# First stage of a two-layer decoder kernel rewritten: pooling bands and weight units take turns, and the router's preparation is spread over the engines

## What is computed

```python
def rmsnorm(x, g):
    y = xf * lax.rsqrt(jnp.mean(xf * xf, axis=-1, keepdims=True) + EPS)
    return (y * g).astype(x.dtype)

def pool_mixer(x, pool_w, pool_scale):          # 4 groups of 512 columns, windows 2, 4, 8, 16
    for gi, w in enumerate(POOL_WINDOWS):
        ...
        outs.append((c - c_prev) / cnt - xf[:, :, gi])      # trailing mean over w rows minus the row
    y = jnp.einsum("bsgc,gcd->bsgd", pooled, pool_w).reshape(B, S, D)
    return y * pool_scale

def hier_moe(x, w_grp, b_grp, w_rt, b_rt, w_gate, w_up, w_down):
    grp_logits = (xt @ w_grp + b_grp)                       # best of 4 groups
    exp_logits = (jnp.einsum("td,gde->tge", xt, w_rt) + b_rt)   # best 2 of its 4 experts
    ...
    h = silu(einsum(xt, w_gate)) * einsum(xt, w_up)         # 16 experts, 2048 -> 512
    return einsum(h * gate, w_down)

def reference(...):
    h = h + pool_mixer(rmsnorm(h, norm_mix[0]), pool_w[0], pool_scale[0])
    h = h + hier_moe(rmsnorm(h, norm_ffn[0]), ...)
    k, v = shared_kv(h, kv_norm, w_kv, k_norm)
    h = h + stick_breaking_layer(rmsnorm(h, norm_mix[1]), k, v, ...)
    h = h + hier_moe(rmsnorm(h, norm_ffn[1]), ...)
```

## Time and profile before

| | us |
|---|---|
| median of 3 runs | 1435.04 (1434.20 to 1435.73) |
| the profiled execution | 1434.92 |
| its span, first to last instruction | 1433.1 |
| TensorE busy | 1351.8 (94%) |
| VectorE busy | 563.1 (39%) |
| ScalarE busy | 423.0 (30%) |
| GpSimd busy | 41.4 (3%) |

### The profile page before, as it was taken

How to read it: one execution, slowest core, us unless ns; L and a number is a source line. 1 busy time by engine, 2 the same in 40 slices (tenths; PEclk the granted TensorE clock), 3 DMA queues, 4 the chain that set the end, 5 groups by cost and what they waited for, 6 DMA issues and landing times.

```text
span 1433.1 us, 22654 instructions
## 1 busy us (share of the span) xinstructions
PE 1351.8 (94%) x9155; PEld 771.8 (54%) x9155; DVE 563.1 (39%) x908; ACT 423.0 (30%) x629; POOL 41.4 (3%) x35
## 2 busy tenths in 40 slices
PE   8899999998998988999999999989999999889896
PEld 7554444443334437888888887774444444344343
DVE  3832232222222226666566665552223223223132
ACT  3511111111101116575656665441111111011110
POOL 0300000000000000101000000010000000000000
PEclk8989999999999998999999999999999999999999
DMA  9979999999999998554554543569999999999995
GB/s 318 377 296 421 420 420 421 421 422 423 422 421 422 422 407 317 183 174 143 179 172 150 174 156 119 194 222 371 420 421 420 422 421 422 421 422 422 422 422 223
DMA packets 95452, 481.79 MB, mean 336 GB/s; under 512 B 9266, under 2 KB 9348, under 8 KB 45988
## 3 DMA queue, kind: packets, MB, share of 16 engines
q1 hardware_dynamic: 94804, 477.59, 83.9%
q10 hardware_dynamic: 432, 2.88, 0.5%
q0 software_dynamic: 160, 0.52, 0.1%
HBM read 478.87 MB, written 2.10 MB: 336 GB/s over the span
## 4 chain that ended last, share of the span: by engine, by line
issue 53%; PE 26%; DMA 15%; DVE 3%; ACT 2%; POOL 1%; SPq 0%; POOLq 0%; DVEq 0%; ACTq 0%
DMA ring<-in_moe_w_up 14%; PE ps L1380 10%; PE ps L1248 6%; PE ps L1415 4%; PE ps L1325 2%; PE ps L1362 1%; POOL head_rs L528 1%; DMA const<-in_constant_table 1%; PE ps L1478 1%; DVE ws L805 1%; PE ps L1363 1%; ACT ws L544 1%; ACT parts L560 1%; DVE xr L833 0%; PE ps L1489 0%
## 5 line engine op out<-in xcount | busy, mean ns | idle before, releaser
L1380 PE MATMUL ps<-ring,xg 128*64 128x512 f32 x1920 | 438.9, 595 | 38.1 <-DMA ring<-in_moe_w_up 37.2
L1248 PE MATMUL ps<-ws,xs 128*128 128x512 f32 x1632 | 384.7, 394 | 5.7 <-DVE xs L1193 2.4
L1248 PEld LDWEIGHTS ps<-ws,xs 128*128 128x128 f32 x1632 | 305.3, 189 | 74.9 <-DVE ws L805 4.2
L1380 PEld LDWEIGHTS ps<-ring,xg 128*64 128x64 f32 x1920 | 141.8, 137 | 304.3 <-issue 304.2
L1415 PE MATMUL ps<-ring,hidT 128*64 128x512 f32 x960 | 212.9, 595 | 0.0
L998 DVE TENSOR_TENSOR y_lo<-ps,y_hi 64x512 fp32r<-64x512 f32 x128 | 88.1, 689 | 218.9 <-ACT y_hi L595 215.9
L808 DVE SCALAR_TENSOR_TENSOR ws<-ring,vecs,ws 128x512 fp32r<-128x512 f32 x192 | 134.3, 748 | 89.5 <-ACT ws L547 89.5
L547 ACT ACTIVATE ws<-ring,vecs 128x512 fp32r<-128x512 f32 x192 | 127.3, 715 | 93.0 <-PE ps L1248 84.6
L978 DVE TENSOR_TENSOR resid<-resid,ps 128x512 f32<-128x512 f32 x128 | 82.7, 684 | 167.9 <-PE ps L1363 167.7
L595 ACT ACTIVATE y_hi<-ps 64x512 fp32r<-64x512 f32 x128 | 75.7, 591 | 239.1 <-PE ps L1415 236.8
L1415 PEld LDWEIGHTS ps<-ring,hidT 128*64 128x64 f32 x960 | 66.2, 137 | 121.5 <-issue 120.0
(11 more groups left out here) (163 smaller groups left out, 685.8 us busy)
## 6 DMA issues: line engine op xcount, KB each, us to landing
ring<-in_moe_w_gate SPq DMA_DIRECT2D x120, 1024.0 KB, 19.7
ring<-in_moe_w_up SPq DMA_DIRECT2D x120, 1024.0 KB, 21.7
ring<-in_moe_w_down SPq DMA_DIRECT2D x120, 1024.0 KB, 21.8
ring<-in_w_kv SPq DMA_DIRECT2D x32, 1024.0 KB, 5.4
ring<-in_w_q SPq DMA_DIRECT2D x16, 1024.0 KB, 5.0
ring<-in_w_o SPq DMA_DIRECT2D x16, 1024.0 KB, 5.0
extra<-in_moe_w_gate SPq DMA_DIRECT2D x8, 1024.0 KB, 9.9
extra<-in_moe_w_up SPq DMA_DIRECT2D x8, 1024.0 KB, 10.0
```

Of the source, the lines that this page charges most:

```text
L1248: last = mm(ps[:, bank + t, :], xs[:, px, k, cols], ws[:, b, pw, j, :], start=(first and j == 0 and n == 0), stop=(last_unit and j == 1 an ...
L1380: last = mm(ps[CAP * h:CAP * h + CAP, b, :], xg[:, b, k, :], both[h][:, j, :], start=(k == 0), stop=(k == KD - 1))
```

## The change

The bands lose columns that are always zero (the second block of 128 columns of a band's upper half becomes 16, `REACH`), so that the first matmul of a band step has 144 columns and not 256, and the band table is smaller. The constant table is split: its first 356 columns are loaded at once, the other 640 after the first weights of attention, and a block of 128 ones is dropped. The router weights are loaded as 80 rows on 80 partitions, and turned in 8 transposes; the norm vector is multiplied into them once (L1137), so that the router rows are plain copies, half by ScalarE and half by VectorE. Norm gains and biases come as a few rows that TensorE spreads, and no longer by transfers in pieces of 16 to 64 bytes. On all engines the band steps and the units now take turns, and the parts of the residual stand in another order, in layer 0 and at the end of layer 1's attention. 16 more rounds of `keep_clock` stand ahead of the bands.

```diff
-C_ID, C_TRI, C_ONE, C_NSUF, C_NONE, C_ADD = 0, 128, 256, 384, 512, 640
-C_IOTA = C_ADD + ZC
+C_ID, C_TRI, C_IOTA = 0, 128, 256
 C_TIE = C_IOTA + CAP
 C_STACK = C_TIE + 16
-C_END = C_STACK + 20
-BANDS = NG * 3 * P
+C_EARLY = C_STACK + 20
+C_NSUF, C_NONE, C_ADD = C_EARLY, C_EARLY + 128, C_EARLY + 256
+C_END = C_ADD + ZC
+REACH = 16
+BAND = P + REACH + P
...
-        WARM_START, WARM_ROUTE, WARM_PICK = 56, 8, 5
+        WARM_START, WARM_BANDS, WARM_ROUTE, WARM_PICK = 56, 16, 8, 5
+        BAND_BANKS = (0, 1, 2, 3, 0, 1, 6, 7)
...
             load(0, pool_w_v[0])
+            sp.dma_start(route_rows[0:KD, :, :], w_grp.rearrange("l (k p) g -> k l (p g)", p=P)).then_inc(route_loaded, 16)
+            for l in range(2):
+                sp.dma_start(route_rows[KD:5 * KD, l, :], w_rt[l].rearrange("g (k p) e -> (g k) (p e)", p=P)).then_inc(route_loaded, 16)
+            sp.dma_start(gain_rows[:, :], norm_ffn.rearrange("l (q c) -> (l q) c", q=NBLK)).then_inc(route_loaded, 16)
...
-            for l in range(2):
-                sp.dma_start(ffn_gain[:, l, :].rearrange("p (q j) -> p q j", j=4),
-                             norm_ffn[l].rearrange("(q p j) -> p q j", q=NBLK, j=4)).then_inc(smalls_loaded, 16)
-                sp.dma_start(bias[:, l, 0:4], b_grp[l:l + 1, :].to_broadcast([P, 4])).then_inc(smalls_loaded, 16)
...
+            def router_rows(l, c):
+
+                act.wait_ge(turned, TURN_ROUTE[l] + 2 * c + 1)
+                nc.scalar.activation(xr[:, 4 * c:4 * c + 2, :],
+                                     ps[:, turn_bank(l, c), :].rearrange("p (k t) -> p k t", k=2),
+                                     ACT.Copy).then_inc(xr_act, 1)
...
+            for t in range(NT):
+                square(1, 3, t)
+            router_rows(1, 3)
+            first(1, 3, 0)
+            logits_out(1)
+            first(1, 3, 1)
+            second(1, 3, 0)
+            second(1, 3, 1)
             moe(1)
...
+                dve.wait_ge(turned, TURN_ROUTE[l] + 2 * c + 2)
+                nc.vector.tensor_copy(xr[:, 4 * c + 2:4 * c + 4, :],
+                                      ps[:, turn_bank(l, c) + 1, :].rearrange("p (k t) -> p k t", k=2)).then_inc(xr_dve, 1)
...
+            def route_weights():
+
+                pe.wait_ge(route_loaded, ROUTES)
+                for l in range(2):
+                    rows = route_rows[:, l, :].rearrange("r (p e) -> r e p", e=4)
+                    for e in range(4):
+                        nc.tensor.transpose(ps[:, 6 + l, 80 * e:80 * e + 80], rows[:, e, :], const[0:80, C_ID:C_ID + 80])
...
+            keep_clock(WARM_BANDS)
+            for b in range(4):
+                bands_in(b)
+            route_weights()
+            pe.wait_ge(vec_done, VECS)
+            pool_units(0)
+            for b in (4, 5):
+                pe.wait_ge(xs_lo, b - 3)
+                bands_in(b)
+            pool_units(1)
...
```

More of the change, by code:

```diff
@@ L438, in moe @@
                     sp.nop()
[L441 to L443 removed]
+            sp.dma_start(vec_rows[V_MIX:V_Q + KD, :], norm_mix.rearrange("l (k p) -> (l k) p", p=P)).then_inc(table_loaded, 16)
+            sp.dma_start(const[:, 0:C_EARLY], table[:, 0:C_EARLY]).then_inc(table_loaded, 16)
@@ L516, in _ @@
             inverse_rms(0)
-            for g in range(2, NG):
-                pool.wait_ge(mixed_done, 2 * (g - 2) + 2)
-                pool.dma_start(scale_row[:, g % 2, :], pool_scale[:, g * BLK:(g + 1) * BLK].to_broadcast([P, BLK])).then_inc(scale_loaded[g], 16)
-            residual_parts(0)
+            load_scale(2)
+            residual_parts(0, 0)
+            load_scale(3)
+            residual_parts(0, 1)
+            left(0, 2)
+            inverse_rms(1)
+            third(0, 2, 1)
+            left(0, 3)
+            third(0, 3, 1)
             inverse_rms(2)
@@ L528, in _ @@
                     nc.gpsimd.tensor_tensor(hr, hs, half[:, :], ALU.pow).then_inc(head_rs_done, 1)
-            residual_parts(1)
+            for c in range(NBLK - 1):
+                residual_parts(1, c)
+            last_parts(1)
         @block.scalar
@@ new lines, in _ @@
+            pool_unit(7)
+            second(0, 0, 0)
+            second(0, 0, 1)
+            squares_and_first(0, 1)
+            router_rows(0, 1)
+            second(0, 1, 0)
+            second(0, 1, 1)
+            square(0, 2, 0)
+            square(0, 2, 1)
+            first(0, 2, 0)
+            router_rows(0, 2)
+            square(0, 3, 0)
+            router_rows(0, 3)
+            square(0, 3, 1)
+            second(0, 2, 0)
+            logits_out(0)
+            second(0, 2, 1)
@@ L639, in _ @@
+            first(0, 2, 1)
+            first(0, 3, 0)
+            first(0, 3, 1)
+            second(0, 3, 0)
+            second(0, 3, 1)
             moe(0)
@@ new lines, in _ @@
+            mean_square(0, True)
+            dve.wait_ge(rs_done, 1)
+            dve.wait_ge(band_loaded, 16)
+            scaled_band(0)
+            dve.wait_ge(vec_turned, 1)
+            nc.vector.tensor_copy(vecs[:], ps[:, 4, 0:V_END]).then_inc(vec_done, 1)
+            for g in range(1, NG):
+                scaled_band(g)
+            dve.wait_ge(vec_done, VECS)
+            nc.vector.tensor_scalar(vecs[:, V_END - 1:V_END], vecs[:, V_END - 1:V_END], HD ** -0.5, None, ALU.mult)
+            nc.vector.tensor_copy(counters[:, 0, :], tri)
@@ new lines, in _ @@
+            third(0, 0)
+            mixed_in(1, 0)
+            mixed_in(1, 1)
+            pooled_lo(6)
+            pooled_lo(7)
+            pool_unit(6)
+            router_rows(0, 0)
+            pool_unit(7)
+            left(0, 1, 0)
+            third(0, 1)
+            router_rows(0, 1)
+            mixed_in(2, 0)
+            mixed_in(2, 1)
+            mixed_in(3, 0)
+            mixed_in(3, 1)
+            router_rows(0, 2)
+            router_rows(0, 3)
+            left(0, 2, 0)
@@ L1081, in _ @@
+            third(0, 2)
+            mean_square(1, False)
+            left(0, 3, 0)
+            third(0, 3)
+            dve.wait_ge(vec_done, BIASES)
             moe(0)
```

329 lines of the change are left out of this document (179 added, 150 removed).

## The result

The changed kernel takes 1414.36 us (median of 4 executions, 1413.23 to 1415.70) against 1435.19 before (4 executions, 1434.20 to 1435.73): ratio 0.9856, 95% interval 0.9839 to 0.9873, so 20.8 us or 1.4% less. Run again beside later experiments (e11), it took 1414.25. Forecast were 1418.9 us and 16.1 us less: the sign came out, the size is 4.7 us short, and the time lies 0.1 us under the low end of the whole range, 1414.5, outside the forecast's own range of 1417.5 to 1420.5. The layer's stream of weights is the bound that the prediction named; what ends the first stage is not, as the experiments show.

The account below looks back on a forecast made before the run. The prediction took layer 0's expert-weight stream as the bound: 15.8 us regained in transfers plus 0.3 in layer 1's router gave 16.1 us less, 1418.9 us by the median, with a range of 1414.5 to 1424.

Parts of the forecast that it names:

- What is bound by what: Layer 0's mixture ends when its weight stream ends, so a shift of that stream shifts the end one for one.
- With no idle stretch the transfers have the 17 slots full at 71.1 us.: First stage: TensorE frees the first slot at 68.6 us, 2.5 us before the transfers need it.
- an idle stretch of the transfers ahead of the first reload: Layer 0's first stage: one of the signs listed beforehand as showing the forecast wrong.
- The terms for the transfers outside the full slots: Before the mixture: smaller tables 1.6 us, dropped gain and bias transfers 0.9, router rows on 80 partitions 0.5.
- TensorE's layout: First stage laid out by hand with old durations: last router block 53.2 us, scaled logits 56.5, first reload 68.6.
- the sum with the wrong bound, 15.8: First stage, transfer time won back: 12.8 us from full slots, plus 1.6, 0.9 and 0.5.
- GpSimd and VectorE lock each other out: Layer 0's splits: at 1.90 us each, parts end at 61.4, reload at 70.1; sum and sign unchanged.
- Layer 1: Router: the logits copy stands behind less ScalarE work, so the mixture starts 0.3 us earlier; bounds 0 and 1.1.
- B: First stage's new chain is longer than laid out; gain 13.9 us down to 9, 1421 to 1426 us; chance 0.26.
- C: Router rows return up to 3.3 us more, or layer 1's router keeps full clock; 1415 to 1417.5 us; chance 0.19.
- D: First stage's engines work in lockstep without overlap, reload at 110 us; slower, 1459 us; chance 0.03.
- E: Layer 0: TensorE only waits earlier for the same stream, slots fill as before; 1432 to 1435 us; chance 0.02.

Follow-up runs that it names:

- e11: The changed kernel itself, run once more beside the other experiments; 1414.25 us (1412.93 to 1416.92).
- e1: Changed kernel with the first stage's old order of work on TensorE, ScalarE and VectorE; new loads, tables, narrow bands and transposes stay; 1425.43 us.
- e2: Changed kernel with the router weights loaded into 16 partitions again and turned in 40 transposes; 1427.17 us.
- e8: Changed kernel with 160 small matmuls as a delay ahead of layer 0's first gather; 1428.90 us.
- e5: Changed kernel with a shorter way from layer 0's last router rows to the gather, by reordered work on VectorE, ScalarE and TensorE; 1413.09 us.
- e3: Changed kernel without the 32 small warm matmuls before the first band (WARM_BANDS 16 to 0); 1414.55 us.
- e4: Changed kernel with 40 small matmuls as a delay ahead of layer 0's first gather; 1414.61 us.
- e7: Changed kernel with the router rows and logits copy of layer 1's last block done as in the kernel before; 1416.33 us.
- e6: Changed kernel with ScalarE's squares and first parts of layer 1 waiting for both row tiles again; 1416.44 us.
- e9: Kernel before, with only layer 1's squares in the output projection waiting for their own row tile; 1432.31 us, ratio 0.9987 to before.
- e10: e5 plus small warm matmuls behind both layers' logits (20 more) and ahead of the output projection's seventh unit (32 more); 1414.17 us.
- e12: e10 with the same warm stretches written in fewer, wider matmuls (256 columns instead of 128); 1410.52 us, ratio 0.9828 to the kernel before.

## Why the prediction was right, and what failed in it

- **What is bound by what.** Right. The mixture of layer 0 ends when its stream ends; 18.02 us at the reload are 17.83 at the last expert, and 12.5, 7.4, 8.5 and 1.0 us in e1, e2, e8 and e5 arrive there within 0.15.
- **"With no idle stretch the transfers have the 17 slots full at 71.1 us."** This step failed. They were full at about 67.5 (reload less the dry time ahead of it: 67.4 to 68.1 in e3, e4, e7, e8 and e11), and 1.2 us of idle lie around the reload at 67.86. So the transfers were not the bound of the first stage; TensorE was, and its chain set the 18.0 us (e4, e5, e8 and the table). The prediction had named its own sign of this, an idle stretch of the transfers ahead of the first reload. It also let the reload come as late as the slots are full, while behind a late reload another 1.3 to 1.5 us pass dry (e3, e4, e7, e8).
- **Why 71.1 was too late.** The terms for the transfers outside the full slots were sized 3.0 us where they give some 6.5. Of the window at 14 us, 2.8 us came back (175 to 354 GB/s), not 0.5; e2 gives 2.1 of it and of its neighbours to the 16 partitions. I had bounds of 0 and 3.8 and took the value next to zero with the argument that the count of pieces stays. From 20.5 to 28 us another 0.6 came back; the rest, some 0.6 us, is spread over windows that I had not counted as lost (352 GB/s at 48 to 52 and 279 at 58 to 60 us before) and was not tested by itself.
- **TensorE's layout.** Right to about 1 us: reload at 68.6 forecast, 67.86 measured, `lg` 56.5 and 56.33, route weights' end 20.3 and 19.2, last router block 53.2 and 53.4. The layout by hand was the better half of the forecast; had it been taken as the bound, the first stage would have come out at 17.3 us. That the sum with the wrong bound, 15.8, came within 2.2 us of the measured 18.0 is in part luck: the two ends lay close together.
- **GpSimd and VectorE lock each other out.** The last third was done at 59.56 (59.6 forecast). VectorE's split took 1.93 us at 42.16, beside GpSimd's of 1.91, and 1.08 at 52.52; what was behind them had room.
- **Layer 1.** The term was 0.3 us with bounds 0 and 1.1; 0.7 were measured at the router, 0.5 of them for the logits and the halved rows (e7). Left out altogether were the squares: 1.6 us in the output projection and 0.3 to 0.4 behind it (e6, e9). I had read the new `square` as the old loop in another shape and not compared its wait.
- **Small misreadings, without weight in the sum.** The late constants are 640 columns, 0.33 MB and not 0.39. In the strip of before, slices 15 (407) and 28 (371) are not at 420 to 423, and attention goes down to 119 GB/s.
- **Rivals.** B (longer chain) did not happen, though its slow units did in e7 (7.35 us for the first two). C comes nearest, 1415 to 1417.5, and the time is 0.6 us better still; its reason that the router's rows give more is right (2.1 us in e2). Its other reason, a clock that stays full through layer 1's router, was wrong: it was 0.72 over the gather there, worth 0.5 us against 0.63 before, and 0.64 from 60 to 64 us in layer 0. D and E fell; with the old order (e1) the slots do fill up long before TensorE reads, and the queue is dry for 13 us.

## What to carry to other kernels

When a chain and a stream run side by side, work out both end times with their errors before naming the bound: here they were measured less than 1 us apart, and the one with the loose term was taken. A small transfer that an engine meets in order (biases behind router rows) costs not its bytes but its landing. Before a shift of a microsecond between two traces is put down to an edit, look how far the same event moves between traces in which nothing was edited there: here 2.1 us. Of a rewritten helper compare every wait, also for the loops that seem untouched. And when a good edit loses, look for a gap without a releaser behind a jump: the length of the program may have done it, as e10 and e12 suggest.

## What the runs showed of the hardware

**Instructions arrive in blocks.** At the start of attention TensorE's program jumps over the part for overfull experts. All kernels wait 5.0 to 5.6 us there for nothing that the trace names. In the seven traces read for it (before, changed, e2, e4, e8, e10, e12) the instruction queue moves one piece of 0.016 MB between 3 and 2 us ahead of the first transpose, and one more between 3 and 4 us behind its start. Where a second wait is seen, work goes on 5.8 to 6.1 us after the first transpose, for example 527.68 and 533.47; 535.50 and 541.33 (e2); 535.90 and 541.73 (e8); 525.92 and 531.70 (e10); 525.99 and 532.08 (e12). What it costs goes with how much work stands before the second wait: 32 transposes in the changed kernel (0.73 us left), 13 in e10 (2.80), 2 in e2 and e8 (5.14). Each matmul has a weight load beside it, so e10 has 40 more instructions ahead than the changed kernel, e2 has 64 and e8 320. From e10 to e2, 24 instructions, the boundary moved by 11 matmuls, or 22; and e8, with 256 more than e2, has it in the same place. By the same count e4, with 80 more, has its boundary ahead of the transposes, and e3, with 64 fewer, has it well behind them; neither shows a second wait. The Trainium skill, page "Runtime: NRT & Kernel Launch", section "Instruction fetch mechanics", gives blocks of 16 KiB or 256 instructions, and a fetch by DMA when a taken branch leads out of the pages at hand; these numbers agree. It calls the crossing of a block "mostly hidden", and behind a jump here it was not. Only e12 was built to test this as the cause; the rest is a count that fits.

**The clock behind a wait.** Behind the same wait of 2.37 us the same 24 matmuls took 5.73 to 5.78 us in the changed kernel, e1, e2, e3, e5 and e11, and 7.19 to 7.37 before and in e4, e6, e7, e8 and e9. The 1.5 us between before and changed at 860 us are therefore not known to be the change's. The first two units of the first stage do the same: 5.68 to 5.75 us in eight of the nine traces that share that part of the first stage, 7.35 in e7. With small matmuls in the wait (e10, e12) they took 5.74 and 5.73. From TensorE's last matmul to the span's end it was 5.0 to 6.7 us, without relation to the edits; the 1.2 us that the table loses there are of that kind.
